# Per-head normalisation of a q/k projection: head sums as two rounded products, scaled units in PSUM, each unit's steps over four loop bodies

## What is computed

```python
h = rms_norm(x, g_pre)
proj = jnp.einsum('btd,de->bte', h, w_in)
q, k, v, gate = jnp.split(proj, SPLIT_C, axis=-1)          # 1024, 256, 256, 1024 columns
q = rms_norm(q.reshape(B, T, 16, 64), q_norm)              # mean of squares over the 64 of a head
k = rms_norm(k.reshape(B, T, 4, 64), k_norm)
q = jnp.concatenate([rope(q[..., :32], rows), rope(q[..., 32:], cols)], axis=-1)   # k alike
```

## Time and profile before

| | us |
|---|---|
| median of three runs (2073.53 to 2073.78) | 2073.57 |
| the profiled execution | 2073.06 |
| its span, first to last instruction | 2071.3 |
| mean granted TensorE clock, share of full speed | 0.995 |

### The profile page before, as it was taken

How to read it: one execution, slowest core, us unless ns; L and a number is a source line. 1 busy time by engine, 2 the same in 40 slices (tenths; PEclk the granted TensorE clock), 3 DMA queues, 4 the chain that set the end, 5 groups by cost and what they waited for, 6 DMA issues and landing times.

```text
span 2071.3 us, 25101 instructions
## 1 busy us (share of the span) xinstructions
PE 2019.8 (98%) x9286; PEld 1618.1 (78%) x9286; DVE 1222.9 (59%) x1920; ACT 1124.4 (54%) x1422; POOL 945.3 (46%) x479
## 2 busy tenths in 40 slices
PE   8999998999999999999999999999999999999997
PEld 6878886888888877777887667888777777777885
DVE  5432145325776767663659878524577778776454
ACT  6142234435666666666445444344577778888431
POOL 1222224435555555656102556433576666667401
PEclk9999999999999999999999999999999999999999
DMA  5133468627655653734335232262233343332534
GB/s 200 52 126 128 153 243 321 170 69 157 129 121 110 164 127 81 163 81 162 108 117 185 92 112 107 102 189 93 80 69 82 75 122 72 81 76 91 172 114 150
DMA packets 171054, 261.36 MB, mean 126 GB/s; under 512 B 78690, under 2 KB 87522, under 8 KB 170932
## 3 DMA queue, kind: packets, MB, share of 16 engines
q1 hardware_dynamic: 170932, 259.76, 44.1%
HBM read 161.78 MB, written 97.92 MB: 125 GB/s over the span
## 4 chain that ended last, share of the span: by engine, by line
PE 89%; ACT 3%; DVE 3%; POOL 2%; issue 1%; DMA 1%; DVEq 0%; SPq 0%; ACTq 0%; POOLq 0%
PE SA L1914 13%; PE OP L1960 10%; PE SM L1840 5%; PE SM L2013 5%; PE SA L533 5%; PE OP L1967 5%; PE OP L533 5%; PE SA L2013 5%; PE OP L1078 4%; PE SA L1078 3%; PE OS L533 3%; PE OS L1960 3%; PE OS L1078 2%; PE OS L2013 2%; PE SM L1836 2%
## 5 line engine op out<-in xcount | busy, mean ns | idle before, releaser
L2370 POOL TENSOR_TENSOR c_PL<-c_PF,c_PH 128x1024 fp32r<-128x1024 f32 x128 | 307.7, 2407 | 137.6 <-ACT c_PH L2090 79.9
L2370 POOL TENSOR_TENSOR ab_PL<-ab_PF,ab_PH 128x1024 fp32r<-128x1024 f32 (+3 forms) x128 | 264.7, 2068 | 192.1 <-ACT ab_PH L2090 135.7
L2087 ACT ACTIVATE ab_PF<-SA 128x1024 f32<-128x1024 f32 (+3 forms) x160 | 143.7, 898 | 158.0 <-PE SA L1875 84.7
L2087 ACT ACTIVATE c_PF<-SA 128x1024 f32<-128x1024 f32 x160 | 164.6, 1029 | 84.6 <-PE SA L1914 83.2
L2170 DVE TENSOR_REDUCE c_MH<-SM 128x1 f32<-128x512 f32 x256 | 170.8, 683 | 66.4 <-PE SM L1840 66.3
L431 POOL TENSOR_TENSOR e_wl<-e_raw,e_wh 128x1024 fp32r<-128x1024 f32 (+1 forms) x31 | 73.7, 2376 | 191.3 <-ACT e_wh L600 191.3
L2090 ACT ACTIVATE c_PH<-c_PF 128x1024 fp32r<-128x1024 f32 x128 | 135.8, 1061 | 4.1
L1914 PE MATMUL SA<-c_Q,c_KA 128*128 128x512 f32 x320 | 127.8, 399 | 3.3 <-ACT c_PF L2087 3.3
L1914 PE MATMUL SA<-c_Q,c_KB 72*128 72x512 f32 x320 | 127.1, 397 | 0.0
L1840 PE MATMUL SM<-c_KA,c_Q 128*128 128x512 f32 x320 | 125.1, 392 | 0.0
L1010 POOL TENSOR_TENSOR n_wl<-n_raw,n_wh 128x1024 fp32r<-128x1024 f32 (+1 forms) x24 | 53.4, 2226 | 150.8 <-ACT n_wh L1175 150.8
(11 more groups left out here) (507 smaller groups left out, 5866.6 us busy)
## 6 DMA issues: line engine op xcount, KB each, us to landing
c_Q<-qC_hi SPq DMA_DIRECT2D x32, 384.0 KB, 4.9
e_raw<-in_w_tiles SPq DMA_DIRECT2D x20, 512.0 KB, 4.0
n_raw<-in_w_tiles SPq DMA_DIRECT2D x20, 512.0 KB, 3.9
e_XF<-in_xT SPq DMA_DIRECT2D x12, 512.0 KB, 10.6
silu_gate<-e_ta SPq DMA_DIRECT2D x24, 256.0 KB, 2.2
ab_Q<-qA_hi SPq DMA_DIRECT2D x16, 384.0 KB, 5.3
ab_G<-silu_gate SPq DMA_DIRECT2D x24, 256.0 KB, 3.9
ab_res<-in_xT SPq DMA_DIRECT2D x24, 256.0 KB, 3.0
```

The lines of the kernel that those rows point to most:

```text
L2087: nc.scalar.activation(used(PF[p], h, s), used(SA, h, s), ACT.Exp).then_inc(e_done, 1)
L2370: nc.gpsimd.tensor_tensor(used(PL[p], h, s), used(PF[p], h, s), used(PH[p], h, s).bitcast(F32), ALU.subtract).then_inc(p_lo[0], 1)
```

## The change

- The squares are written twice by ACT: plain (`tsq`) and rounded (`tsh`). DVE takes the difference (`low_square`, into `tsl`), and the head sums become two float32r matmuls, of `tsh` and of `tsl`, by a rounded copy `selr` of `headsel` that ACT makes once in body 4.
- Logarithm and exponential are written in place into the SM bank. `finish` is cut into `turn` (the addition) and `scale` (the multiplication), and `scale` writes into PSUM, into banks OS and MT in turn, for all q/k units but the last two. `high` and `low` read there. `products` of the q/k units get four accumulators instead of six.
- The order moves. DVE body n is now: `low(n - 4)`, `scale(n - 3)`, `turn(n - 1)`, `evict(n)` and the shuffle, `low_square(n)`. ACT body n: weights, `head_scale(n - 3)`, `high(n - 3)`, both squares of n. PE: head sums of n - 2 behind `products(n)` from unit 11 on, two of them at 8 (units 4, 5), 10 (7, 8) and 33 (31, 32); those of 33 within the first pass of the values. SP stores unit n - 4, and three stores stand ahead of the loads of the value weights.

The diff, without the hunks that name semaphores and with short context:

```diff
@@ -822,7 +823,7 @@
     W = [("x", 10 + t, 8, D) for t in range(2)] + [("x", t, 8, D) for t in range(10)] + [
         ("values", u, 2, 512) for u in range(4)] + [("x", t, 8, D) for t in (12, 13, 14, 15, 16, 10, 17, 11)]
-    EARLY, CATCH = 4, 20
+    EARLY = 4
     U = [(tiles[t], t, c) for c in ORDER[0:2] for t in range(2)]
@@ -857,6 +858,16 @@
         return (i + 1) % 3
+    def sums_after(n):
+
+        if n in (8, 10):
+            return (4, 5) if n == 8 else (7, 8)
+        if n == 9:
+            return (6,)
+        if n > 10:
+            return (n - 2, n - 1) if n == v0 - 1 else (n - 2,)
+        return ()
+
     def stored_before(i):
@@ -893,7 +905,9 @@
     sl = [at(f"sl{i}", [P, CH], F32, SPLIT_LO + 8192 + 2048 * i) for i in range(4)]
     tsq = [at(f"tsq{i}", [P, CH], F32, SPLIT_LO + 16384 + 2048 * i) for i in range(2)]
-    tsd = [at(f"tsd{i}", [P, CH], F32, REST + 16384 + 2048 * i) for i in range(2)]
+    tsl = [at(f"tsl{i}", [P, CH], F32R, SPLIT_LO + 16384 + 2048 * i) for i in range(2)]
+    tsh = [at(f"tsh{i}", [P, CH], F32R, REST + 16384 + 2048 * i) for i in range(2)]
+    selr = at("headsel_r", [P, P], F32R, SPLIT_LO + 20480)
     sq_at = ([HALF0 + 24576, HALF1 + 28672], [SET[1] + 4096, SET[1] + 6144],
@@ -917,7 +931,15 @@
     def bank_of(n):
+        if 4 <= n < v0:
+            return n % 4
         return (n + 2) % 6 if n < gate0 else late_bank(n, gate0, N, (4, 3, 2, 1, 0))
+
+    SCALED = len(qk) - 2
+
+    def scaled(i):
+
+        return acc[4 + i % 2] if i < SCALED else ta[place_of(i)][:]
@@ -971,11 +993,16 @@
             sp.dma_start(tables[i][:], A["sinC" if i % 2 else "cosC"]).then_inc(tab_in, 16)
         for n in range(N):
+            if n == v0:
+                for m in range(v0 - 4, v0 - 1):
+                    store(m)
             for w in begins[n]:
                 if 1 < w < len(W) - 2:
                     load(sp, w + 2)
-            if n - 2 in qk:
-                store(n - 2)
+            if n - 4 in qk and n < v0:
+                store(n - 4)
+            if n == v0:
+                store(v0 - 1)
             if kind[n] == "value":
@@ -1035,7 +1062,7 @@
             pool.wait_ge(tab_done, 2 + b)
             pool.wait_ge(r_swap, i + 1)
-            pool.wait_ge(q_sq, i + 1)
+            pool.wait_ge(q_hi, i + 1)
             nc.gpsimd.tensor_tensor(ta[s][:], ta[s][:], tables[b][:, pc], ALU.mult).then_inc(r_cos, 1)
@@ -1104,12 +1131,14 @@
             i = qk.index(n)
             if i == 0:
-                pe.wait_ge(tab_in, 96)
+                pe.wait_ge(sel_set, 1)
             if i < 3:
                 pe.wait_ge(deviation, 3 - i % 2)
-            pe.wait_ge(q_sq, i + 1)
-            wait_count(pe, q_log, i - 1)
-            nc.tensor.matmul(sums[i % 2], sel[:], tsq[i % 2][:], start=True, stop=True).then_inc(q_sum, 1)
+            pe.wait_ge(q_hi, i + 1)
+            wait_count(pe, r_norm, i - 1)
+            nc.tensor.matmul(sums[i % 2], selr[:], tsh[i % 2][:], start=True, stop=False)
+            pe.wait_ge(q_lo, i + 1)
+            nc.tensor.matmul(sums[i % 2], selr[:], tsl[i % 2][:], start=False, stop=True).then_inc(q_sum, 1)
@@ -1117,11 +1146,13 @@
                 b = w % 2
                 pe.wait_ge(w_lo, w + 1)
-                if q == 1:
-                    head_sums(v0 - 1)
                 for i in range(TT):
                     if q == 0 and i % 2 == 0:
-                        pe.wait_ge(acc_read, n0 + i // 2 - 5)
+                        wait_count(pe, acc_read, last_user(bank_of(n0 + i // 2), n0) + 1)
+                    if q == 0 and i == 6:
+                        head_sums(v0 - 1)
+                    if q == 0 and i == 8:
+                        pe.wait_ge(lo_done, SCALED)
                     c, tok = token_tile(i)
@@ -1160,8 +1191,7 @@
                 x_square_sum(min(n // 2, 2))
             if n < v0:
-                for m in {8: (4, 5), CATCH: (n - 3, n - 2), v0 - 1: (n - 2, n - 1)}.get(
-                        n, (n - 3 + n // CATCH,) if n > 8 else ()):
+                for m in sums_after(n):
                     head_sums(m)
@@ -1221,16 +1251,15 @@
             wait_count(act, q_sum, i - 1)
             nc.scalar.activation(tsq[i % 2][:], ta[place_of(i)][:], ACT.Square).then_inc(q_sq, 1)
+            nc.scalar.activation(tsh[i % 2][:], ta[place_of(i)][:], ACT.Square).then_inc(q_hi, 1)
         def head_scale(n):
             i = qk.index(n)
             act.wait_ge(q_sum, i + 1)
-            wait_count(act, r_norm, i - 1)
-            nc.scalar.activation(tsd[i % 2][:], sums[i % 2], ACT.Ln, bias=epst[:], scale=1.0 / HD
-                                 ).then_inc(q_log, 1)
+            nc.scalar.activation(sums[i % 2], sums[i % 2], ACT.Ln, bias=epst[:], scale=1.0 / HD).then_inc(q_log, 1)
             act.wait_ge(q_log, i + 1)
-            nc.scalar.activation(tsd[i % 2][:], tsd[i % 2][:], ACT.Exp, scale=-0.5).then_inc(q_rstd, 1)
+            nc.scalar.activation(sums[i % 2], sums[i % 2], ACT.Exp, scale=-0.5).then_inc(q_rstd, 1)
@@ -1238,7 +1267,7 @@
             if n in qk:
                 act.wait_ge(r_norm, qk.index(n) + 1)
-                nc.scalar.activation(out, ta[place_of(qk.index(n))][:], ACT.Copy).then_inc(hi_done, 1)
+                nc.scalar.activation(out, scaled(qk.index(n)), ACT.Copy).then_inc(hi_done, 1)
                 return
@@ -1254,14 +1283,20 @@
                 root(act, 2)
             for w in splits[n]:
-                if w > 4:
+                if 4 < w < V0 + 2 or n > v0:
                     high_weights(act, w)
-            if n - 1 in qk:
-                head_scale(n - 1)
+            if n == EARLY:
+                act.wait_ge(tab_in, 96)
+                nc.scalar.activation(selr[:], sel[:], ACT.Copy).then_inc(sel_set, 1)
+            for m in range(n - 3, n) if n == v0 else (n - 3,):
+                if m in qk and n <= v0:
+                    head_scale(m)
+                    high(m)
+            if n == v0:
+                for w in splits[v0][1:]:
+                    high_weights(act, w)
             if n in qk:
                 square(n)
-            if n - 1 in qk:
-                high(n - 1)
             if kind[n] == "value":
@@ -1310,7 +1345,7 @@
         if qk.index(n) < 3:
             dve.wait_ge(g_stored[s], 32 if s == 0 else 16)
-        wait_count(dve, lo_done, qk.index(n) - 2)
+        wait_count(dve, r_norm, qk.index(n) - 2)
         nc.vector.tensor_tensor(ta[s][:], bank(n), rstd[:, cols(c)], ALU.mult).then_inc(acc_read, 1)
@@ -1352,31 +1387,56 @@
                                         ALU.mult, ALU.mult).then_inc(tab_done, 1)
-        def finish(n):
+        def low_square(n):
+
+            i = qk.index(n)
+            dve.wait_ge(q_hi, i + 1)
+            nc.vector.tensor_tensor(tsl[i % 2][:], tsq[i % 2][:], tsh[i % 2][:].bitcast(F32), ALU.subtract
+                                    ).then_inc(q_lo, 1)
+
+        def turn(n):
             i = qk.index(n)
             s = place_of(i)
             dve.wait_ge(r_cos, i + 1)
             dve.wait_ge(r_sin, i + 1)
-            dve.wait_ge(q_sq, i + 1)
+            dve.wait_ge(q_hi, i + 1)
             nc.vector.tensor_tensor(ta[s][:], ta[s][:], tb[s][:], ALU.add).then_inc(r_sum, 1)
+
+        def scale(n):
+
+            i = qk.index(n)
             dve.wait_ge(r_sum, i + 1)
             dve.wait_ge(q_rstd, i + 1)
-            nc.vector.tensor_tensor(ta[s][:], ta[s][:], tsd[i % 2][:], ALU.mult).then_inc(r_norm, 1)
+            wait_count(dve, lo_done, i - 1)
+            if i < 2:
+                dve.wait_ge(acc_read, 4)
+            nc.vector.tensor_tensor(scaled(i), ta[place_of(i)][:], sums[i % 2], ALU.mult).then_inc(r_norm, 1)
         def low(n):
             i = qk.index(n)
             dve.wait_ge(r_norm, i + 1)
             dve.wait_ge(hi_done, i + 1)
-            nc.vector.tensor_tensor(sl[stage_of(n)][:].bitcast(F32R), ta[place_of(i)][:], sh[stage_of(n)][:],
+            nc.vector.tensor_tensor(sl[stage_of(n)][:].bitcast(F32R), scaled(i), sh[stage_of(n)][:],
                                     ALU.subtract
                                     ).then_inc(lo_done, 1)
         for n in range(N):
             if n == v0:
-                finish(n - 1)
-                low(n - 2)
-                low(n - 1)
+                low(n - 4)
+                scale(n - 3)
+                turn(n - 1)
+                low(n - 3)
+                for m in (n - 2, n - 1):
+                    scale(m)
+                    low(m)
+            if n in qk:
+                if n - 4 in qk:
+                    low(n - 4)
+                if n - 3 in qk:
+                    scale(n - 3)
+                if n - 1 in qk:
+                    turn(n - 1)
             if n >= gate0:
@@ -1384,10 +1444,8 @@
                 for k in range(1, KT)[3 * (n - 1):3 * n]:
                     add_square(dve, 2, k)
-            if n - 1 in qk and n != v0:
-                finish(n - 1)
-            if n - 2 in qk and n < v0:
```

(9 more changed lines are left out.)

## The result

| | before, us | after, us |
|---|---|---|
| median | 2073.55 (18 runs) | 2077.11 (18 runs) |
| the profiled execution | 2073.06 | 2078.83 |
| its span | 2071.3 | 2077.0 |
| busy: PE / DVE / ACT / POOL | 2019.8 / 1222.9 / 1124.4 / 945.3 | 2016.1 / 1209.3 / 1136.4 / 941.2 |

What follows compares the result with a forecast made beforehand. The prediction took PE to bound the late q/k stage before, and a DVE-ACT-POOL ring after; 4.0 us there plus 1.9 in the tail made +5.9, 2079.5 us, range 2066 to 2085.

Steps and rivals of the forecast that it cites:

- The ring: q/k stage: evict, squares, POOL's rotation, turn, next evict wait on each other; 19.5 us for three units against PE's 17.9.
- plain step: q/k stage, evict to next evict without weights or table scalings between: 5.79 us, 19 such steps.
- The weights: POOL's low_weights take the shared port ahead of turn, which then takes 2.81 us: eight q/k steps of 7.9 us.
- The half-sized weights: Step into unit 31, where POOL's weights are half as large (1.27 us against 2.41): 6.8 us.
- The table scalings: Step into unit 9: two DVE scalings wait for POOL at the shared port, 7.9 us; beside POOL it were 6.0.
- The tail: Last q/k evict to second value pass: 10.4 us against 8.5 before, through turn(33) held by value weights, then low(31).
- Sum: First to last q/k evict 187.9 us against 183.9, plus 1.9 in the tail: +5.9 us.
- Rival 2: q/k stage and tail: table scalings beside POOL (-1.9), steps of 5.7 (-1.7), shorter tail (-1): +1.5, 2075 us; chance 0.2.
- Rival 1: Weights don't hold turn: q/k steps would be 5.79, PE the bound at 5.95; -14 us, 2059; chance 0.17.
- Rival 3: DVE's scale and low cost up to 1.8 us with PSUM, plain q/k steps 6.9: 2100 us; chance 0.05.
- PE's pauses: q/k stage up to 1320 us: PE gaps of about 1.5 us for every three units, each ended by scale.
- PE's new bound: PE's price per q/k unit with rounded head sums: 5.95 us, 0.40 less than the 6.35 before.

Runs made afterwards that it cites:

- e1: The changed kernel with turn(n - 1) on DVE moved behind evict(n) and the shuffle; 2055.41 us, 0.9914 of the kernel before.
- e6: The changed kernel with a third, unread square of each q/k unit on ACT, between evict and the rotation; 2092.58 us, 1.0093 of the kernel before.
- e7: The changed kernel with a second, unread rounding copy of each scaled unit on ACT, ahead of high; 2077.31 us, 1.0019 of the kernel before.
- e2: The changed kernel with one added wait: POOL starts the weights' low half only after turn of the unit before; 2062.21 us, 0.9946 of the kernel before.
- e5: e1 with the second pair of table scalings moved from body 8 to body 20; 2051.25 us, 0.9891 of the kernel before.
- e4: The kernel before with only the rounded head sums, second square and low_square added, in the old order; 2085.17 us, 1.0052 of the kernel before.
- e8: The changed kernel with scaled units in two SBUF tiles instead of two PSUM banks; 2090.02 us, 1.0076 of the kernel before.

## Why the prediction was right, and where it was off

- **The ring** was named with its members, and e1, e6 and e7 show it. The timelines of one plain step, DVE, ACT and POOL:

```profile
1187.09 0.68 DVE L1349 TENSOR_TENSOR n_ta<-OP,n_rstd 128x512 f32<-128x512 f32 x1
...
1189.00 0.69 DVE L1394 TENSOR_TENSOR n_tsl<-n_tsq,n_tsh 128x512 fp32r<-128x512 f32 x1 [0.43 <-ACT n_tsh L1254]
...
1192.18 0.69 DVE L1404 TENSOR_TENSOR n_ta<-n_ta,n_tb 128x512 f32<-128x512 f32 x1 [1.27 <-POOL n_tb L1067]
```

```profile
1187.81 0.63 ACT L1253 ACTIVATE n_tsq<-n_ta 128x512 f32<-128x512 f32 x1 [1.90 <-DVE n_ta L1349]
1188.35 0.61 ACT L1254 ACTIVATE n_tsh<-n_ta 128x512 fp32r<-128x512 f32 x1
1188.87 0.64 ACT L1260 ACTIVATE SM<-SM,epst 128x512 f32<-128x512 f32 x1
1189.54 0.58 ACT L1262 ACTIVATE SM<-SM 128x512 f32<-128x512 f32 x1
```

```profile
1189.13 1.71 POOL L1066 TENSOR_TENSOR n_ta<-n_ta,n_table 128x512 f32<-128x512 f32 x1 [2.74 <-ACT n_tsh L1254]
1190.80 1.29 POOL L1067 TENSOR_TENSOR n_tb<-n_tb,n_table 128x512 f32<-128x512 f32 x1
```

  From the start of `evict`, `low_square` ends at 2.60 where I had 2.67, the first rotation at 3.75 (3.82), the second at 5.00 (5.08), `turn` starts at 5.09 (5.18), the next `evict` at 5.70 (5.79). Nearly the whole difference, 0.07 of 0.09, is one term: DVE reacted to ACT in 0.04 us (1188.96 to 1189.00), not in the 0.11 that I took from a single pair. `low_square` so leaves the port earlier, and all that follows moves with it. The 19 plain steps average 5.68, which makes 2.0 us, two thirds of the error.
- **The weights**: 7.82 on average where I had 7.9, by the same 0.09; `turn` took 2.82, and 2.81 in the single meeting before. 0.7 us of the error. The half-sized weights gave 6.71 for 6.8.
- **The table scalings**: 7.66 for 7.9. One row shows both instructions together with POOL beside them:

```profile
1168.47 3.42 DVE L1387 TENSOR_SCALAR n_table<-n_table,n_head_gain 128x1024 f32<-128x1024 f32 x2
```

  Where POOL was idle but for the last 0.3 us (from 1139.82), two took 1.41. The Trainium skill's rule on the shared port pair (SBUF — State Buffer, "SBUF: two separate sides"), by which a one-input instruction in a two-port mode takes part too, is borne out by this row.
- **The tail**: 10.65 us from the last `evict` to the second pass, forecast 10.4. It was made as forecast: `turn(33)`, held by the value weights, ends 6.8 us after the last `evict`, `low(31)` 7.4 after it, and the ninth tile waits for that; the four tiles then take 3.1 and not 2.9. The wait of the head sums of 33 for `scale(31)` did not show (they start at 1330.86 without idle time); PE's long wait is one step earlier, of the head sums of 32 for `scale(30)`, and ends before the pass begins:

```profile
1324.33 0.76 PE L1139 MATMUL SM<-n_tsh,n_headsel_r 128*128 128x512 f32 x1 [4.97 <-DVE OS L1414]
...
1333.56 0.36 PE L1162 MATMUL OS<-n_wh,n_XH 128*128 128x256 f32 x1 [0.66 <-DVE n_sl L1420]
```

  `turn(33)` in DVE's timeline:

```profile
1331.11 1.70 DVE L1404 TENSOR_TENSOR n_ta<-n_ta,n_tb 128x512 f32<-128x512 f32 x1 [0.76 <-POOL n_tb L1067]
```
- **Sum**: 187.9 forecast from the first `evict` to the last, 184.9 measured, and +5.9 became +3.6. So the steps' order was right and the sizes 1 to 2% too long; with the ring and the old pace so close (6.4 and 6.34 us a unit), that decides between "slower by over 0.2%" (my 0.56) and "within" (my 0.26). The measured +3.6 us is 0.17%, just under my +4 to +9, and the interval of the ratio, [1.0011, 1.0023], holds the 0.2% line, so the runs don't settle which of the two it is.
- **Rival 2** (a ring slightly shorter, +1.5) came true in one of its three terms: the plain steps are 5.7, but the table scalings did not run beside POOL and the tail was not shorter. Its terms add up to +1.3, not +1.5.
- **Rival 1** (DVE wins the port, 2059) stands 3 us from what e2 gave when a wait made DVE win, 2062: its price was nearly right, its condition not met. **Rival 3** (PSUM as destination dear) fell: `scale` into PSUM takes 0.70.
- **PE's pauses** were forecast at 1.5 us for three units; the bracketed idle times add up to 0.9 to 1.0. The ring gives 19.2 against PE's 17.7, so 1.5 is lost. But there are two pauses in three units, not three; a matmul's row lasts 0.39 where the next one starts after 0.23, so each pause hides 0.16 of itself, and the first matmul behind it takes 0.08 more until the next. That makes 1.4 of the 1.5.
- **Also off**: PE's new bound, 5.95 a unit by the prediction, is 5.89 in e1 and e5, since the 24 matmuls take 5.44 behind rounded head sums and not 5.49; the saving is 0.46 a unit and not 0.40. And for e4 I gave too little weight to the chain through DVE.

## What to carry to other kernels

When a step is moved across an in-order queue, look for rings: if work that waits for unit n - 1's last stage now stands ahead of unit n's first stage, the stages' latencies add up to the pace, however idle each engine is. Sum the ring once from rows, with its meetings at the port between DVE and POOL, and compare it with the bound engine's price per unit; saving on the bound engine while lengthening the ring (here 0.46 us of PE a unit bought with one more square and one more difference) gains nothing. An operand placed in PSUM takes a DVE instruction out of that contest: `low` takes 0.68 us in the changed kernel, 1.78 in e8.

## What the runs showed of the hardware

- At the port the one that starts first went first. POOL's next instruction starts 0.04 us before the end of the last, and DVE, woken by that last one, reacts 0.09 to 0.10 after it, so POOL had the port in every meeting of weights and `turn`. Where DVE's instruction was already waiting, it went ahead of POOL's next one: in e8 `low`, from 1254.72, ends at 1256.50, and POOL's rotation, from 1255.91, only at 1257.64.
- Whoever waits for the port finishes sooner after the release than its full time: POOL 1.15 us after DVE's end against 1.29 alone, DVE 0.56 us after POOL's end (`low` in e8) against 0.68.
- ACT in place in PSUM is a little faster than into SBUF: logarithm 0.64 and exponential 0.58 us, in e4, which leaves them as before, 0.69 and 0.63.
- Two rounded matmuls of the head sums take 0.46 us of PE's time (0.23 each in the chain of e1), one plain float32 product 0.86.
